# Eight of eleven down units in seven products, with GpSimd making three of four sums of weight blocks

## The reference

```python
def swiglu(h, w_gate, w_up, w_down):
    return (jax.nn.silu(h @ w_gate) * (h @ w_up)) @ w_down

for l in range(DEPTH):                      # DEPTH = 2
    x = x + 0.5 * swiglu(rms_norm(x, norm_w[l, 0]), ffn_w_gate[l, 0], ffn_w_up[l, 0], ffn_w_down[l, 0])
    h = rms_norm(x, norm_w[l, 1])
    x = x + (mixer_mla_gdn(h, ...) if l % 2 == 0 else mixer_spatial_gating(h, ...))
    x = x + 0.5 * swiglu(rms_norm(x, norm_w[l, 2]), ffn_w_gate[l, 1], ffn_w_up[l, 1], ffn_w_down[l, 1])
```

## Time and profile before

| | before |
|---|---|
| median of 3 runs | 1071.8 us (1069.93 to 1072.92) |
| the profiled execution | 1071.83 us, span 1070.0 us |
| TensorE, matmul | 1049.0 us (98% of the span) |
| VectorE | 813.6 us (76%) |
| ScalarE | 564.1 us (53%) |
| GpSimd | 46.4 us (4%) |
| granted clock of TensorE | 1.00 |
| mean DMA rate | 173 GB/s |

### The profile page before, as it was taken

One profiled execution on the slowest core, in us unless ns is written; L12 is line 12 of the kernel. 1 busy time (PEld: TensorE's weight loads), 2 busy tenths in 40 slices (PEclk: granted clock), 3 DMA queues, 4 the chain that ended last, 5 costly groups with the idle time before them and its releaser, 6 DMA issues.

```text
span 1070.0 us, 19233 instructions
## 1 busy us (share of the span) xinstructions
PE 1049.0 (98%) x8325; PEld 961.9 (90%) x8325; DVE 813.6 (76%) x1071; ACT 564.1 (53%) x695; POOL 46.4 (4%) x32
## 2 busy tenths in 40 slices
PE   8999999999789999999999999999999999999998
PEld 8999987898678899999789999878888889999986
DVE  5876789899853686768988777898665647766797
ACT  6644446585764554445655444565665436444451
POOL 1000000110162000000000000000000000000000
PEclk9999999999999999999999999999999999999999
DMA  9755556563000665565546655566655456565551
GB/s 308 232 188 171 193 197 187 165 197 119 1 4 18 222 197 178 179 196 194 199 158 197 196 170 186 198 199 223 191 169 182 166 156 213 176 196 176 180 195 40
DMA packets 127214, 184.91 MB, mean 173 GB/s; under 512 B 4221, under 2 KB 101738, under 8 KB 127002
## 3 DMA queue, kind: packets, MB, share of 16 engines
q1 hardware_dynamic: 126384, 181.85, 52.6%
q0 software_dynamic: 448, 1.71, 0.5%
q10 hardware_dynamic: 298, 0.12, 0.0%
HBM read 182.62 MB, written 1.05 MB: 172 GB/s over the span
## 4 chain that ended last, share of the span: by engine, by line
PE 80%; DVE 14%; issue 4%; ACT 2%; ACTq 0%; DVEq 0%
PE banks L1514 22%; PE banks L1516 22%; PE banks L1515 22%; DVE wlo L958 3%; DVE arena L1030 2%; DVE rounded L1038 2%; PE banks L1957 2%; DVE raw L1032 1%; DVE arena L1031 1%; PE banks L1676 1%; PE banks L1677 1%; PE banks L1675 1%; DVE wlo L1040 1%; PE banks L1592 1%; PE banks L1593 1%
## 5 line engine op out<-in xcount | busy, mean ns | idle before, releaser
L950 DVE TENSOR_TENSOR wlo<-raw,whi 128x2048 fp32r<-128x2048 f32 (+1 forms) x142 | 322.4, 2281 | 106.5 <-ACT whi L498 106.4
L1514 PE MATMUL banks<-xTh,whi 128*128 128x256 f32 x1392 | 394.6, 283 | 2.0 <-DVE wlo L1173 1.8
L498 ACT ACTIVATE whi<-raw 128x2048 fp32r<-128x2048 f32 (+1 forms) x170 | 311.0, 1842 | 160.2 <-PE banks L1516 143.5
L1516 PE MATMUL banks<-xTh,wlo 128*128 128x256 f32 x1392 | 393.9, 283 | 0.0
L1515 PE MATMUL banks<-xTl,whi 128*128 128x256 f32 x1392 | 393.9, 283 | 0.0
L1514 PEld LDWEIGHTS banks<-xTh,whi 128*128 128x128 f32 x1392 | 267.2, 192 | 3.0 <-issue 2.5
L1515 PEld LDWEIGHTS banks<-xTl,whi 128*128 128x128 f32 x1392 | 267.2, 192 | 0.0
L1516 PEld LDWEIGHTS banks<-xTh,wlo 128*128 128x128 f32 x1392 | 267.2, 192 | 0.0
L1514 PE MATMUL banks<-whi,hTh 128*128 128x512 f32 (+1 forms) x192 | 77.8, 405 | 1.3 <-DVE wlo L1040 1.0
L1516 PE MATMUL banks<-whi,hTl 128*128 128x512 f32 (+1 forms) x192 | 74.7, 389 | 0.0
L1515 PE MATMUL banks<-wlo,hTh 128*128 128x512 f32 (+1 forms) x192 | 74.6, 388 | 0.0
(11 more groups left out here) (289 smaller groups left out, 1529.9 us busy)
## 6 DMA issues: line engine op xcount, KB each, us to landing
raw<-in_ffn_w_down SPq DMA_DIRECT2D x44, 1024.0 KB, 4.9
raw<-in_ffn_w_gate SPq DMA_DIRECT2D x43, 1024.0 KB, 5.4
raw<-in_ffn_w_up SPq DMA_DIRECT2D x43, 1024.0 KB, 5.4
raw<-in_sg_w_in SPq DMA_DIRECT2D x16, 1024.0 KB, 5.5
raw<-in_ab_w_in SPq DMA_DIRECT2D x8, 1024.0 KB, 5.1
raw<-in_sg_w_out SPq DMA_DIRECT2D x8, 1024.0 KB, 4.9
raw<-in_ab_w_out SPq DMA_DIRECT2D x4, 1024.0 KB, 5.0
raw<-in_ab_w_in SPq DMA_DIRECT2D x2, 832.0 KB, 4.4
```

What stands on the lines that cost most here:

```text
L498: A(whi[:, j % SLOTS, 0:n], raw[:, j % RAW_SLOTS, 0:n], ACT.Copy).then_inc(S("hi_ready"), 1)
L950: TT(wlo[:, j % RAW_SLOTS, 0:n], raw[:, j % RAW_SLOTS, 0:n], whi[:, j % SLOTS, 0:n].bitcast(f32), ALU.subtract).then_inc(S("lo_ready"), 1)
L1514: mm(out_ap, lh, rh, start=first, stop=False)
L1516: return mm(out_ap, ll, rh, start=False, stop=last)
```

## The change

`SEVEN` grows from six to eight units, d+1 to d+8; d, d+9 and d+10 stay plain. GpSimd gets a function `right_sums(f)` that makes the additions of 1024 and 512 columns for all eight units of a sublayer; VectorE keeps the addition into block 3, now the first step of `base_lo`. The sums have three buffers; the third lies where f_row, `gate` and `prod` lie, so that it waits for the last rest of the products. ScalarE rounds the sums in two steps. The left sums come ahead of the rounding of the product; three of their four blocks have buffers (384 columns), the fourth is written into `prod` in place and is rounded with it. TensorE waits for a unit's base rests first and, before its fourth product (in the last unit its second), for the rest of the sums and of block 3. Two semaphores of the first mixer are joined into one.

```diff
-SEVEN = (1, 2, 4, 5, 7, 8)
+SEVEN = (1, 2, 3, 4, 5, 6, 7, 8)
...
-        gate = at(R0 + 4096, 2, 512)
-        prod = at(R0 + 5120, 2, 512)
+        gate = at(R0 + 1024, 2, 512)
+        prod = at(R0 + 2048, 2, 512)
...
-        S_AT = [R0 + o for o in (512, 1536, 2560, 6144, 7168)] + [N0 + 3072]
-        S_SUM = [at(o + 512, 512) for o in S_AT]
-        S_HI, S_LO = [at_r(o, 512) for o in S_AT], [at_r(o + 512, 512) for o in S_AT]
-        T_AT = [N0, XT0 + 1536]
-        T_SUM, T_HI, T_LO = [at(o, 1536) for o in T_AT], [at_r(o, 1536) for o in (N0 + 1536, XT0)], [at_r(o, 1536) for o in T_AT]
+        S_AT = [R0 + 3072 + 768 * i for i in range(7)] + [N0 + 3072]
+        S_SUM = [at(o + 384, 384) for o in S_AT]
+        S_HI, S_LO = [at_r(o, 384) for o in S_AT], [at_r(o + 384, 384) for o in S_AT]
+        T_AT, T_HI_AT = [N0, XT0 + 1536, R0 + 1536], [N0 + 1536, XT0, R0]
+        T_SUM, T_HI, T_LO = [at(o, 1536) for o in T_AT], [at_r(o, 1536) for o in T_HI_AT], [at_r(o, 1536) for o in T_AT]
...
-                return S("sums_lo"), 2 * N7 * (n // N7) + N7 + n % N7 + 1
+                return S("sums_lo"), 3 * N7 * (n // N7) + N7 + 2 * (n % N7) + 1
...
+            def right_sums(f):
...
+                add = lambda o, a, b: nc.gpsimd.tensor_tensor(o, a, b, ALU.add)
+                for k in range(N7):
+                    j, n = u_ffn[f] + 22 + SEVEN[k], 2 * (N7 * f + k)
+                    pool.wait_ge(S(f"raw_loaded{j % RAW_SLOTS}"), 16 * arrivals[j])
+                    if k == 1:
+                        pool.wait_ge(S("unit_done"), u_ffn[f] + 22)
+                    elif k == 2:
+                        pool.wait_ge(S("prod_lo"), PAIRS_F * (f + 1))
+                    elif k > 2:
+                        pool.wait_ge(S("unit_done"), u_ffn[f] + 23 + SEVEN[k - 3])
+                    b = raw[:, j % RAW_SLOTS, :].rearrange("p (b n) -> p b n", n=512)
+                    t3 = T_SUM[k % 3].rearrange("p (b n) -> p b n", n=512)
+                    add(t3[:, 0:2, :], b[:, 1:3, :], bc(b[:, 3:4, :], [P, 2, 512])).then_inc(S("t_summed"), 1)
+                    pool.wait_ge(S("t_summed"), n + 1)
+                    add(t3[:, 2, :], t3[:, 1, :], b[:, 1, :]).then_inc(S("t_summed"), 1)
...
             after(mul(qkn_q[:, 0:NOPE], qkn_q[:, 0:NOPE], qkn_k[:, 0:NOPE]))
+            right_sums(0)
+            if stop_after == "ffn0":
+                return
...
+            right_sums(1)
+            right_sums(2)
             pool.wait_ge(S("x_updated"), 16)
...
                                     ALU.mult).then_inc(S("ws_masked"), 1)
+            right_sums(3)
...
             def prod_hi(f, c):
...
-                act.wait_ge(S("prod_ready"), n + 1)
+                if c in SEVEN:
+                    act.wait_ge(S("summed"), 2 * N7 * f + SEVEN.index(c) + 1)
+                else:
+                    act.wait_ge(S("prod_ready"), n + 1)
...
             def left_hi(f, k):
...
-                act.wait_ge(S("summed"), 2 * N7 * f + k + 1)
...
             def right_hi(f, k):
...
+                n = 2 * (N7 * f + k)
+                act.wait_ge(S("t_summed"), n + 1)
+                A(T_HI[k % 3][:, 0:1024], T_SUM[k % 3][:, 0:1024], ACT.Copy).then_inc(S("sums_hi"), 1)
+                act.wait_ge(S("t_summed"), n + 2)
+                A(T_HI[k % 3][:, 1024:1536], T_SUM[k % 3][:, 1024:1536], ACT.Copy).then_inc(S("sums_hi"), 1)
...
-                A(T_HI[k % 2], T_SUM[k % 2], ACT.Copy).then_inc(S("sums_hi"), 1)
...
             def ffn(f):
                     if c in SEVEN:
...
-                right_hi(f, 1)
-                hi(d + 4)
-                hi(d + 5)
-                right_hi(f, 2)
-                hi(d + 6)
-                right_hi(f, 3)
-                hi(d + 7)
-                hi(d + 8)
-                right_hi(f, 4)
-                hi(d + 9)
-                right_hi(f, 5)
-                hi(d + 10)
+                for k in range(1, N7):
+                    right_hi(f, k)
+                    hi(d + 3 + k)
...
             def base_lo(j):
...
+                dve.wait_ge(S("t_summed"), 2 * n + 2)
+                b = raw[:, j % RAW_SLOTS, :].rearrange("p (b n) -> p b n", n=512)
+                TT(b[:, 3, :], T_SUM[n % N7 % 3][:, 1024:1536], b[:, 0, :], ALU.add).then_inc(S("summed"), 1)
...
-                   ALU.subtract)
+                   ALU.subtract).then_inc(S("sums_lo"), 1)
...
             def x_lo(xi, k, norm):
...
-            def left_sums(c, k):
...
+            def left_sums(f, c, k):
...
+                dve.wait_ge(S("prod_ready"), PAIRS_F * f + c + 1)
...
-                TT(d[:, 3, :], a[:, 0, :], d[:, 2, :], ALU.subtract).then_inc(S("summed"), 1)
+                TT(a[:, 3, :], a[:, 0, :], d[:, 2, :], ALU.subtract).then_inc(S("summed"), 1)
...
             def left_lo(f, k):
...
-                dve.wait_ge(S("sums_hi"), 3 * N7 * f + k + 1)
+                dve.wait_ge(S("sums_hi"), 4 * N7 * f + k + 1)
...
-            def right_sums(f, k):
+            def right_lo(f, k):
...
-                dve.wait_ge(S(f"raw_loaded{j % RAW_SLOTS}"), 16 * arrivals[j])
-                if k:
-                    dve.wait_ge(S("unit_done"), u_ffn[f] + (22 if k < 2 else 23 + SEVEN[k - 2]))
-                b = raw[:, j % RAW_SLOTS, :].rearrange("p (b n) -> p b n", n=512)
-                t3 = T_SUM[k % 2].rearrange("p (b n) -> p b n", n=512)
-                link(TT(t3[:, 0:2, :], b[:, 1:3, :], bc(b[:, 3:4, :], [P, 2, 512]), ALU.add))
-                link(TT(t3[:, 2, :], t3[:, 1, :], b[:, 1, :], ALU.add))
-                TT(b[:, 3, :], t3[:, 2, :], b[:, 0, :], ALU.add).then_inc(S("summed"), 1)
...
-            def right_lo(f, k):
...
-                j = u_ffn[f] + 22 + SEVEN[k]
-                dve.wait_ge(S("sums_hi"), 3 * N7 * f + N7 + 2 * k + 1)
-                TT(T_LO[k % 2], T_SUM[k % 2], T_HI[k % 2].bitcast(f32), ALU.subtract)
-                dve.wait_ge(S("sums_hi"), 3 * N7 * f + N7 + 2 * k + 2)
+                n = 4 * N7 * f + N7 + 3 * k
+                dve.wait_ge(S("sums_hi"), n + 2)
+                TT(T_LO[k % 3], T_SUM[k % 3], T_HI[k % 3].bitcast(f32), ALU.subtract)
+                dve.wait_ge(S("sums_hi"), n + 3)
...
                     product(f, c)
+                    if c in SEVEN:
+                        left_sums(f, c, SEVEN.index(c))
...
-                        right_sums(f, 0)
...
                     prod_lo(f, c)
...
-                    if c in SEVEN:
-                        left_sums(c, SEVEN.index(c))
...
-                right_sums(f, 1)
-                base_lo(d + 2)
-                right_lo(f, 1)
-                lo(d + 3)
-                right_sums(f, 2)
-                base_lo(d + 4)
-                right_lo(f, 2)
-                right_sums(f, 3)
-                base_lo(d + 5)
-                right_lo(f, 3)
-                lo(d + 6)
-                right_sums(f, 4)
-                base_lo(d + 7)
-                right_lo(f, 4)
-                right_sums(f, 5)
-                base_lo(d + 8)
-                right_lo(f, 5)
+                for k in range(1, N7):
+                    base_lo(d + SEVEN[k])
+                    right_lo(f, k)
                 lo(d + 9)
                 lo(d + 10)
...
-                t = [a[k % 2].rearrange("p (b n) -> p b n", n=512) for a in (T_HI, T_LO)]
+                t = [a[k % 3].rearrange("p (b n) -> p b n", n=512) for a in (T_HI, T_LO)]
...
-                left = lambda n: [x[:, n, :] for x in s_]
+                left = lambda n: [x[:, n, :] for x in s_] if n < 3 else a(1, 1)
...
                 products = ((a(1, 0), base_(2), 0), (left(2), sum_(2), 1), (left(1), sum_(0), 2), (left(0), sum_(1), 3),
...
                     products = tuple(products[n] for n in (0, 4, 5, 6, 2, 3, 1))
-                for lh, rh, bank in products:
+                for n, (lh, rh, bank) in enumerate(products):
+                    if n == (1 if k == N7 - 1 else 3):
+                        pe.wait_ge(S("sums_lo"), 3 * N7 * f + N7 + 2 * k + 2)
...
                     last = split_mm(B[bank][:], lh[0], lh[1], rh[0], rh[1], own and k == 0, own and k == N7 - 1)
...
```

More of the change, by code:

```diff
@@ L408, in load @@
                 pool.dma_start(dst, src).then_inc(S(name), 16)
-            if stop_after == "ffn0":
-                return
             pool.wait_ge(S("hi_ready"), 1)
@@ L452, in _ @@
             D3 = Dec.rearrange("p (m j) -> p m j", j=64)
-            mul(D3, D3, bc(const("causal").unsqueeze(1), [P, NT * HEADS, 64])).then_inc(S("dec_masked"), 1)
-            per_head(QKVn[2].rearrange("p t n -> p (t n)"), QKVn[2], beta).then_inc(S("vb_ready"), 1)
+            mul(D3, D3, bc(const("causal").unsqueeze(1), [P, NT * HEADS, 64])).then_inc(S("dec_then_vb"), 1)
+            per_head(QKVn[2].rearrange("p t n -> p (t n)"), QKVn[2], beta).then_inc(S("dec_then_vb"), 1)
             def pool_lo(j):
@@ L1418, in _ @@
                 if n == 0:
-                    dve.wait_ge(S("dec_masked"), 1)
+                    dve.wait_ge(S("dec_then_vb"), 1)
```

(2 more changed lines are left out.)

## The result

The changed kernel takes 1132.2 us, the median of five runs (1130.86 to 1133.52), against 1070.2 us before (also the median of five): 1.058 times as long, 95% interval 1.056 to 1.060. The forecast was 1134 us, within 1105 to 1160. The span of its profiled execution is 1131.6 us, against 1070.0, and TensorE's mean granted clock in it 0.979, against 1.00.

A forecast was written before the change was run, and what follows sets the result against it. TensorE, busy 98%, bounds the kernel by its matmuls' sum. GpSimd and VectorE taking turns make each down stage 61.3 us instead of 46.1: 61 us in four, plus 1 us at stage changes, giving 1134 us, range 1105 to 1160.

The forecast's parts named there:

- The collision: Down stages: a VectorE instruction with two SBUF inputs and a GpSimd one reading SBUF never overlap; the later is blocked throughout.
- VectorE's 4.67 us a unit: Down stages: VectorE's remaining addition and three rests per seven-product unit take 4.67 us, against 4.76 us of matmuls.
- GpSimd's price: Down stages: GpSimd's additions of 1024 and 512 columns take 2.4 and 1.2 us, 3.6 us a unit.
- the hidden part: Down stages: two changes of hand between GpSimd and VectorE a unit hide 0.13 us each, 1.8 us a stage.
- The upper bound: Down stages: nothing hidden, 0.1 us lost at each of four hand-overs: 1152 us; with empty stretches about 1160.
- The stage: Each down product, to the start of its last two units: 61.3 us instead of 46.1, +15.2 us.
- Free parts: Left sums' new order, GpSimd's first sum, its queue order, joined semaphore and load timing cost nothing that the next stage awaits.
- Plain matmuls: In the profile after, the line of the plain units' matmuls (1592) shows 80, not 144.
- The signs: Profile after: GpSimd's 1024-column additions often above 4 us, VectorE's 1536-column rests up to 4 on the mean, TensorE's waits some 60.
- The additions of the first unit: GpSimd's first sum falls in the gate and up products, some 18 us ahead of the stage, holding VectorE 3.6 us, free.
- Side by side: Rival, down stages: GpSimd and VectorE overlap as the change wants, nothing waits: -5.4 us, 1066 us; 10%.
- The clock: Rival, down stages: waiting TensorE falls to 1.2 GHz, a unit lasts 9.5 us, +41 us a stage: 1236 us; 4%.

## Why the prediction was right

- **The collision** read from two events holds through all four stages. It was the step that decided; with eight units, the runs with writes (1062 us), copies (1110), additions (1132) and double additions (1224) leave the length of GpSimd's reading instructions as what moves the time. The prediction took both rows for a rule by which the later instruction is held; but in the earlier trace rows VectorE's began 0.02 us before GpSimd's by the trace and was held all the same, so starts that close don't tell which of the two will wait. That the collision needs a read, not two inputs of GpSimd, the prediction had not said; its words "both inputs in SBUF" claimed no more than was needed.
- **VectorE's 4.67 us a unit** is what its list takes where GpSimd is away: 162.62 to 167.27 in the first stage is 4.65.
- **GpSimd's price** was taken as 3.6 us less 0.26 hidden, 3.34. Undisturbed the additions take 2.4 and 1.29 us; what they add to the pair is less: the stage after the first sums, from 143.58 to 200.06, is 56.5 us, of which VectorE's list is 7 x 4.67 + 4.4 = 37.1, so six units of GpSimd take 19.4, 3.2 us each. The 512 columns were reckoned 0.1 us short, the hidden part 0.2 us a unit short; that the two nearly cancel is luck. The upper bound, with losses at each hand-over, was on the wrong side: hand-overs hide time.
- **The stage** was to take 61.3 us from its first matmul to the start of the last two units, in place of 46.1. By that measure it takes 61.4: from 139.12 to 200.56, which is 21 matmuls after unit 8's first at 195.72. **Free parts**: the six-unit kernel with additions on VectorE bears them out. **Plain matmuls**: 80 on line 1593, as said.
- **The signs** that it named went the right way, three of them by less than it said. GpSimd's additions of 1024 columns take 2.82 us on the mean and none reaches 4 (the longest is 3.87), where they were to be often above 4. VectorE's rests of 1536 columns have means of 2.14 and 2.23 us, and 4 us is the length of the longest (3.97), not of a mean. TensorE's waits for line 1054 are 42 us, not some 60: the prediction had the matmuls keep their pace, and some 20 us went into slower matmuls instead.
- **The additions of the first unit** lie at 121.25 to 125.3, 14 to 18 us ahead of the stage. They hold up a rest of VectorE (3.39 us from 124.05, in place of 2.29), for which TensorE doesn't wait.
- **Side by side** would have brought about 1062 us, as the writes show, not 1066. From the start of the first stage to the first transposes of X it takes 49.3 us, before 51.6; two units' matmuls are 1.4 us of these 2.3, and TensorE's small waits of before are gone as well. Whether they are all of the rest wasn't tried.
- **The clock** fell, which the forecast gave 4%, but not as that rival had it. The profile's windows of the changed kernel (us; PE, PEld, DVE, ACT, POOL busy; granted clock, DMA share, GB/s), and the matmuls of the unit in question:

```profile
160.00:165.00 5.00, 2.25 (x5) 1.82 (x6) 4.97 (x4) 1.67 (x2) 2.14 (x1) 0.75 0.21 85
165.00:170.00 5.00, 5.00 (x21) 4.06 (x20) 4.96 (x5) 3.81 (x5) 2.62 (x1) 0.91 0.30 87
```

```profile
162.75 0.80 PE L1513 MATMUL banks<-whi,hTh 128*128 128x512 f32 x1 [3.19 <-DVE wlo L1054]
163.34 0.63 PE L1514 MATMUL banks<-wlo,hTh 128*128 128x512 f32 x1
163.77 0.63 PE L1515 MATMUL banks<-whi,hTl 128*128 128x512 f32 x1
...
166.39 0.39 PE L1513 MATMUL banks<-rounded 128*128 128x512 f32 x1
```

After a wait of 3.2 us the matmuls follow each other every 0.43 us, not 0.23: the lower level, 1.2 GHz. By 166.4 they are back at 2.4 GHz. Its twelve matmuls take 4.3 us, in place of 2.9 from 153.70, so that unit is finished 1.4 us late and GpSimd waits 5.24 us for its place, but VectorE has ready work all that time. The same happened after the wait of 3.21 us before 186.47. From there TensorE doesn't wait again, and it comes to the last two units at 200.56, 0.4 us after VectorE's last plain rest has ended (195.66 + 4.49 = 200.15): that is the most that the clock can have cost in this stage.

The length of the wait alone doesn't tell when the clock falls. It didn't after 3.17 us before 177.41, nor after 2.10 us before 153.70; but it did in the second stage after a wait as short as that one:

```profile
524.37 0.79 PE L1513 MATMUL banks<-whi,hTh 128*128 128x512 f32 x1 [2.09 <-DVE wlo L1054]
524.97 0.63 PE L1514 MATMUL banks<-wlo,hTh 128*128 128x512 f32 x1
525.39 0.63 PE L1515 MATMUL banks<-whi,hTl 128*128 128x512 f32 x1
```

What tells them apart wasn't tried.

## What to carry to other kernels

Idle time of GpSimd is not free time: before work is moved there, count what VectorE has in the same stretch with two inputs in SBUF, and add the lengths instead of taking the greater. Work of GpSimd that only writes SBUF, or that falls where VectorE is idle or has one of its two inputs in PSUM, runs beside it. For the last, besides, there is one instruction of the changed kernel, which keeps its 0.69 us while GpSimd reads SBUF:

```profile
122.05 0.69 DVE L1008 TENSOR_TENSOR arena<-banks,arena 128x512 f32<-128x512 f32 x1 [0.39 <-PE banks L1515]
...
121.25 2.68 POOL L426 TENSOR_TENSOR arena<-raw 128x1024 f32<-128x1024 f32 x1 [98.59 <-DMA raw<-in_ffn_w_down]
```

Two events in a trace were enough to see it: look for an instruction that takes longer than its group, and for what ends when it does.

## What the runs showed of the hardware

- GpSimd's instructions that read SBUF hold up VectorE's with two SBUF inputs, with one input (copies, 1110 us) as with two; its memsets don't, at 3.0 us of them a unit (1062 us).
- With both lists full the engines alternate by instruction, and each of GpSimd's instructions holds VectorE for 0.2 to 0.25 us less than it lasts alone (two additions, 3.7 us alone, cost 3.2 a unit; four copies, 3.3 alone, cost 2.4).
- Alone, GpSimd takes 2.4 us for an addition of 1024 columns of float32 and 1.29 for 512, 1.04 and 0.61 for copies, 0.96 and 0.53 for memsets; VectorE takes 1.22 and 0.69 us for the additions.
- After two of the three waits over 3.1 us in the first stage TensorE's matmuls ran at the lower level for some 3 us. After a wait of 2.1 us they did so in the second stage and not in the first. The granted clock of the two stretches was 0.94 (139.4 to 200.1 us) and 0.89 (510 to 570 us).
